# One of two modulation tables is computed on VectorE and ScalarE inside a feed-forward, instead of on TensorE inside a recurrent branch

## The chip, the cores and the metric

The kernel runs on one core of a Trainium2 chip. The metric is the device time of one execution in microseconds (us). The core has TensorE (matmuls into PSUM banks), VectorE, ScalarE and GpSimd; SyncE issues the weight transfers here. In the profile they are PE (with PEld for weight loads), DVE, ACT, POOL and SP.

## The reference, cut to what matters

Two network blocks of two layers each work one after the other on 256 tokens of width 1024. Block 1 mixes three branches (A is a delta-rule recurrence of many 64x64 products) and has a gated feed-forward. Block 2 modulates its norms and residual gates by tables that depend only on the condition `c`:

```python
cond = jax.nn.silu(c)
for layer in range(DEPTH):
    mod = (cond @ ada_w[layer] + ada_b[layer])[:, None, :]
    sh1, sc1, g1, sh2, sc2, g2 = jnp.split(mod, 6, axis=-1)
    h = rms_norm_2(x, norm_mix_g[layer]) * (1.0 + sc1) + sh1
    x = x + g1 * hybrid_mixer(h, ...)
    h = rms_norm_2(x, norm_ffn_g[layer]) * (1.0 + sc2) + sh2
    y = swiglu(h, ...) if layer % 2 == 0 else moe_swiglu(h, ...)
    x = x + g2 * y
```

`c` is one vector of 1024 and `ada_w[layer]` is 1024 x 6144, 25 MB in float32. The products `cond @ ada_w[0]` and `cond @ ada_w[1]` can be made at any time before block 2 needs them.

## The kernel before, in words

**Units.** All weights stream through the core in units of 128 x 1024 float32 (512 KB), in an order fixed by the table `ORDER.loads`. The SyncE program `weight_program` issues them in that order into a ring of 6 slots. Load n goes into the slot of load n-6 and waits until that older unit has been read for the last time.

**Split units (kind "s").** ScalarE copies a unit into `w_high` in a rounded form (`high_to`, L1713). VectorE makes `w_low` = unit minus `w_high` (`low_to`, L2235), and this frees the ring slot (semaphore `s_low_halves`). TensorE then multiplies high by high, high by low and low by high, 24 matmuls of 256 columns for one unit. There are 6 places for split units in `w_high`, so `high_to` also waits for TensorE to have multiplied the unit 6 before.

**Raw units (kind "r").** These are read by TensorE straight from the ring. In each of block 1's two layers, 48 of them make one modulation table. `mod_point` (L867) is called at 17 or more points of branch A, between its products. A point takes up to 4 raw units, two matmuls each (128 partitions by 32 columns, 512 wide). After each round of 16 units, ScalarE copies the bank out (`full`), a later point transposes it (`turned`, L872) and ScalarE takes the columns (`out`). The next round waits for `out`. At branch A's end VectorE copies the finished 48 columns into `raw_mod`.

**Feed-forward of block 2, layer 0.** Its 66 split units are 22 groups j of two up units and one down unit. TensorE takes up(j), then down(j-2). In group j ScalarE first cuts the units up to `fed_ahead(j)` (three new units for each group from the third on), then makes sigmoid(gate) (L2032), waits for VectorE's products, and rounds the hidden tile (`high`, L2036). VectorE makes the three `w_low`, two products (L2267) and the low part of the hidden tile. Engines work in program order, so a wait holds everything behind it on that engine.

Of the kernel before, what the change touches and what calls it, by code (L numbers as in the profile page):

```python
# [3 lines left out]
P = 128  # L4
# [107 lines left out]


class Order:

# [3 lines left out]
    LAYER1 = FEED + 3 * FF_GROUPS  # L119
    RAW1 = MOD_UNITS + 1  # L120
    QK2, RQK2, RV2, GV2, GR2, RG2, OUT2, FEED2 = 0, 4, 12, 16, 20, 24, 28, 36

    def __init__(self):
        self.loads = []
        for layer in range(LAYERS):
            self._load("s", self.layer1(layer), self.A_V)
            self._load("r", layer * self.RAW1, 1)
            self._load("s", self.layer1(layer) + self.A_V, self.C - self.A_V)
            self._load("r", layer * self.RAW1 + 1, MOD_UNITS)
# [41 lines left out]
    @staticmethod  # L171
    def fed_ahead(j, groups):

        return 5 if j == 0 else min(3 * j + 4, 3 * groups - 1)

    def layer1(self, layer):
# [70 lines left out]

class Rounds:

    ROUND = 2 * KT

    def __init__(self):
        self.taken, self.stage = 0, 0

    def more(self, n):
        r, at = self.stage // 3, self.stage % 3
        if at == 1:
            self.stage += 1  # L260
            return r, True, range(0)
        if at:
            return r, False, range(0)
        first, self.taken = self.taken, min(self.taken + n, (r + 1) * self.ROUND, MOD_UNITS)
        return r, False, range(first, self.taken)

    def out(self):
        r, at = self.stage // 3, self.stage % 3
        if (at == 0 and self.taken == (r + 1) * self.ROUND) or at == 2:
            self.stage += 1  # L270
            return r, at
        return r, None

    def open(self):
        return self.stage < 3 * MOD_UNITS // self.ROUND


STEPS = {
# [6 lines left out]
    "mod_act":  # L285
        "full0 out0 full1 out1 full2 out2",
    "a_pe":
# [14 lines left out]
    "b_pe":  # L302
# [150 lines left out]
def build(nc, a_x, a_pos, a_cond, a_const, a_par1, a_par2, a_router, a_norms, a_weights, a_moe, a_out):  # L453
# [163 lines left out]
    for w in tmps:  # L617
# [48 lines left out]
    CG, CV, SG, HD = ([new(T) for _ in TWO] for _ in range(4))  # L666


    space(0)
# [58 lines left out]
    of_start = stage("start", 0)  # L728
    of_mod, of_a, of_b, of_c, of_merge, of_ffn, of_add = (
        [stage(name, layer) for layer in range(LAYERS)]  # L730
        for name in ("mod", "a", "b", "c", "merge", "ffn", "add"))
    of_mix = [stage("first", 0), stage("mix", 0)]
# [53 lines left out]
    def tensor_program():  # L786
# [80 lines left out]
        def mod_point(M, A, rounds, layer, n=4):  # L867
            r, turn, units = rounds.more(n)
            if turn:
                pe.wait_ge(*M.act(f"full{r}"))  # L870
                for i in range(4):
                    ins = pe.transpose(psum[7][:, i * P:(i + 1) * P], rope[:, i * P:(i + 1) * P], c_("ident"))  # L872
                ins.then_inc(*M.pe.mark(f"turned{r}"))
            for j in units:
                k, block = j % Rounds.ROUND // 2, j % 2
                if j % Rounds.ROUND == 0:
                    pe.wait_ge(*(M.act(f"out{r - 1}") if r else A.dve("kk_scaled")))
                raw = layer * ORDER.RAW1 + 1 + j
                pe.wait_ge(*arrived("r", raw))
                for h in TWO:  # L880
                    q = 2 * block + h
                    ins = mm(psum[7][32 * q:32 * q + 32, :], cond[:, k:k + 1].to_broadcast([P, 32]),
                             weights("r", raw)[:, h * 512:(h + 1) * 512], k == 0, k == KT - 1)
                ins.then_inc(s_raw, 1)
            rounds.out()

        def branch_a(R, A, M, side, layer):
            s0, rounds, VT = ORDER.layer1(layer), Rounds(), PA[:, 8:12, :]
            point = lambda: mod_point(M, A, rounds, layer)
# [40 lines left out]
            ins.then_inc(*A.pe.mark("kk_sum"))  # L930
            low = layer * ORDER.RAW1
            lora = weights("r", low)
# [770 lines left out]
    def scalar_program():  # L1703
# [69 lines left out]
        def branch_a(A, M, side, layer):  # L1773
            s0, a, rounds = ORDER.layer1(layer), A.act, Rounds()
            WA, GD = PA[:, 12, :], PA[:, 13, :]

            def point():
                rounds.more(4)
                r, step = rounds.out()
                if step == 0:  # L1780
                    act.wait_ge(s_raw, layer * ORDER.RAW1 + (r + 1) * Rounds.ROUND + 1)
                    act.activation(rope, psum[7][:, :], Copy).then_inc(*M.act.mark(f"full{r}"))
                elif step == 2:
                    act.wait_ge(*M.pe(f"turned{r}"))
                    src = psum[7][:, :].rearrange("p (i q s) -> p q i s", i=4, q=4)[:, :, :, 0:1]
                    dst = mod[:, 16 * r:16 * r + 16].rearrange("p (q i o) -> p q i o", q=4, o=1)
                    act.activation(dst, src, Copy).then_inc(*M.act.mark(f"out{r}"))
# [31 lines left out]
            tiles_in(10, 14)  # L1819
            act.wait_ge(s_raw, layer * ORDER.RAW1 + 1)  # L1820
            for b in TWO:
# [193 lines left out]

        def feed_forward(F, s0, groups, conv=None, ahead=False, rotary=None):
            for j in range(groups):
# [186 lines left out]
        for layer in range(LAYERS):  # L2204
# [9 lines left out]
            if layer == 0:  # L2214
                feed_forward(of_feed, s0 + ORDER.FEED2, FF_GROUPS, ahead=True)
        route(of_route)
# [9 lines left out]
    def vector_program():  # L2226
# [114 lines left out]
        def branch_a(A, M, side, layer):  # L2341
# [436 lines left out]

        def feed_forward(F, S, s0, groups, conv=None, scale=None, ahead=False, rotary=None):
            for j in range(groups):  # L2780
# [325 lines left out]
        def modulation(S, layer):  # L3106
            d = S.dve
            tt(d, mod, raw_mod[:, layer * MOD_UNITS:(layer + 1) * MOD_UNITS], par2(layer, "ada_b"), ADD)
            prior(d)
# [29 lines left out]
        for layer in range(LAYERS):  # L3139
# [9 lines left out]
            if layer == 0:  # L3149
                feed_forward(of_feed, of_add2, s0 + ORDER.FEED2, FF_GROUPS, scale=lambda dt: mod[:, 40 + dt:41 + dt],  # L3150
                             ahead=True)
        route(of_route)
# [4 lines left out]
    def weight_program():  # L3157
# [3 lines left out]
        for n, (kind, unit) in enumerate(ORDER.loads):  # L3161
# [51 lines left out]
def weight_units(inp):  # L3213
# [3 lines left out]
    for l in range(LAYERS):  # L3217
# [3 lines left out]
        index = np.concatenate([c[:, 1024:1092], np.zeros((D, 60), np.float32)], 1)  # L3221
        mod = inp["ada_w_2"][l].reshape(KT, P, MOD_UNITS // KT, UNIT).transpose(2, 0, 1, 3).reshape(MOD_UNITS, P, UNIT)
        gates = columns(w[:, B_END + 1092:])
        raw += [low] + [mod[2 * KT * r + KT * b + k] for r in range(3) for k in range(KT) for b in range(2)]
        a_units = columns(w[:, :A_END])
# [7 lines left out]
    for l in range(LAYERS):  # L3233
# [7 lines left out]
    assert len(split) == ORDER.experts and len(raw) == LAYERS * ORDER.RAW1  # L3241
    return np.stack([(split if kind == "s" else raw)[n] for kind, n in ORDER.loads if kind == "r" or n < ORDER.experts])

# [67 lines left out]
```

## Time and profile before

| | |
|---|---|
| median of 3 runs | 2488.91 us (2483.47 to 2493.6) |
| the profiled execution's own time | 2488.56 us |
| its span | 2487.1 us |
| TensorE busy | 2289.8 us, 92% of the span |
| VectorE busy | 1600.5 us, 64% |
| ScalarE busy | 1177.9 us, 47% |
| weights and constants read | 423.08 MB |

Busy time is an average over stages with different limits: what an edit is worth is read in its own stage. In lists of instructions, the bracket at the end is the idle time of the engine just ahead of the row, with what ended it. A float32 matmul appears as two rows, so `x16` for raw units is 4 units.

### The profile page before, as it was taken

What the parts mean: (1) busy time and instruction counts of PE and PEld (TensorE: products, weight loads), DVE (VectorE), ACT (ScalarE), POOL (GpSimd) and SP (SyncE); (2) the same over time, 40 slices, a digit from 0 to 9 for tenths busy, and PEclk for the clock granted to TensorE, in tenths of its full rate; (3) what the DMA queues carried; (4) which work ended last, traced back from release to release, by engine and by line L of the source; (5) the groups of instructions that cost most, each with busy time, mean ns of one, the idle gap of its engine ahead of it and who ended that gap; (6) DMA issues with size and microseconds to landing.
All of it is one profiled execution on the core that took longest, in us unless ns stands there. A gap on an engine that the chain in (4) does not pass through costs nothing.

```text
span 2487.1 us, 44944 instructions
## 1 busy us (share of the span) xinstructions
PE 2289.8 (92%) x19043; PEld 2067.2 (83%) x19043; DVE 1600.5 (64%) x2429; ACT 1177.9 (47%) x1713; POOL 0.2 (0%) x4
## 2 busy tenths in 40 slices
PE   7889788999999888889999989999989999999998
PEld 7569788999976788888998979998978888887776
DVE  6537776687772687576875756555755554477886
ACT  5234534455552354355554435444434443356665
POOL 0000000000000000000000000000000000000000
PEclk9999898999999999899998979999978999999999
DMA  5664333355457533243653415563412455578895
GB/s 204 226 250 160 114 107 114 127 197 195 143 181 265 185 119 111 93 161 128 204 188 110 136 51 179 182 190 129 136 35 102 169 181 184 195 248 325 321 331 196
DMA packets 118635, 427.06 MB, mean 172 GB/s; under 512 B 13345, under 2 KB 16161, under 8 KB 118305
## 3 DMA queue, kind: packets, MB, share of 16 engines
q1 hardware_dynamic: 116016, 421.81, 49.5%
q8 instruction: 150, 2.46, 0.4%
q10 hardware_dynamic: 2416, 2.37, 0.3%
q14 instruction: 53, 0.43, 0.1%
HBM read 423.08 MB, written 1.05 MB: 171 GB/s over the span
## 4 chain that ended last, share of the span: by engine, by line
PE 75%; DVE 15%; ACT 5%; issue 3%; DMA 2%; SPq 0%; ACTq 0%; DVEq 0%
PE bank L790 74%; DVE w_low L2235 5%; DVE arena L2267 4%; DVE arena L2276 2%; DMA ring<-in_weights 1%; ACT w_high L1713 1%; DVE y_mix L2267 1%; DVE arena L2748 1%; DVE arena L2273 1%; PE bank L1599 1%; ACT arena L1986 1%; DVE small L2746 0%; DVE arena L2286 0%; DVE arena L2271 0%; ACT arena L1931 0%
## 5 line engine op out<-in xcount | busy, mean ns | idle before, releaser
L2235 DVE TENSOR_TENSOR w_low<-ring,w_high 128x1024 fp32r<-128x1024 f32 x700 | 823.3, 1220 | 159.4 <-ACT w_high L1713 159.0
L1713 ACT ACTIVATE w_high<-ring 128x1024 fp32r<-128x1024 f32 x700 | 700.3, 1051 | 166.2 <-PE bank L790 159.3
L790 PE MATMUL bank<-u_high,w_high 128*128 128x256 f32 x2576 | 745.9, 290 | 34.9 <-DVE u_low L2267 24.0
L790 PE MATMUL bank<-u_low,w_high 128*128 128x256 f32 x2576 | 737.3, 286 | 0.0
L790 PE MATMUL bank<-u_high,w_low 128*128 128x256 f32 x2576 | 736.5, 286 | 0.0
L790 PEld LDWEIGHTS bank<-u_high,w_high 128*128 128x128 f32 x2576 | 502.1, 195 | 48.3 <-issue 40.0
L790 PEld LDWEIGHTS bank<-u_low,w_high 128*128 128x128 f32 x2576 | 501.8, 195 | 0.1
L790 PEld LDWEIGHTS bank<-u_high,w_low 128*128 128x128 f32 x2576 | 500.9, 194 | 0.0
L790 PE MATMUL bank<-arena 64*64 64x64 f32 (+5 forms) x4456 | 245.1, 252 | 76.9 <-issue 20.1
L790 PEld LDWEIGHTS bank<-arena 64*64 64x64 f32 (+2 forms) x4456 | 215.0, 156 | 115.1 <-issue 60.6
L2267 DVE TENSOR_TENSOR arena<-arena 128x256 f32<-128x256 f32 (+3 forms) x218 | 141.8, 666 | 46.7 <-ACT arena L2030 21.3
L790 PE MATMUL bank<-w_high,u_high 128*128 128x256 f32 (+1 forms) x480 | 164.9, 344 | 0.0
L790 PE MATMUL bank<-w_high,u_low 128*128 128x256 f32 (+1 forms) x480 | 162.6, 339 | 0.0
L790 PE MATMUL bank<-w_low,u_high 128*128 128x256 f32 (+1 forms) x480 | 162.3, 338 | 0.0
L790 PE MATMUL bank<-hid_high,w_high 128*128 128x256 f32 x528 | 147.7, 280 | 0.9 <-DVE w_low L2235 0.9
L790 PE MATMUL bank<-hid_low,w_high 128*128 128x256 f32 x528 | 147.3, 279 | 0.0
L790 PE MATMUL bank<-hid_high,w_low 128*128 128x256 f32 x528 | 147.3, 279 | 0.0
L2267 DVE TENSOR_TENSOR turned_low<-bank,turned_high 128x256 fp32r<-128x256 f32 (+1 forms) x66 | 24.9, 400 | 158.7 <-ACT turned_high L2142 158.7
L2142 ACT ACTIVATE turned_high<-bank 128x256 fp32r<-128x256 f32 (+1 forms) x66 | 22.2, 365 | 220.8 <-PE bank L1599 220.8
L1719 ACT ACTIVATE arena<-bank 128x512 f32<-128x512 f32 (+1 forms) x72 | 42.1, 585 | 164.7 <-PE bank L790 164.6
L2276 DVE SCALAR_TENSOR_TENSOR arena<-bank,params,arena 128x255 f32<-128x255 f32 (+1 forms) x204 | 85.5, 476 | 42.8 <-ACT arena L2028 26.2
L790 PE MATMUL bank<-w_high,turned_high 128*128 128x512 f32 x242 | 99.6, 412 | 8.5 <-DVE w_low L2235 7.1
(294 smaller groups left out, 3068.6 us busy)
## 6 DMA issues: line engine op xcount, KB each, us to landing
ring<-in_weights SPq DMA_DIRECT2D x534, 512.0 KB, 4.5
ring<-in_moe SPq DMA_DIRECT2D x264, 512.0 KB, 5.3
const<-in_const SPq DMA_DIRECT2D x1, 2619.0 KB, 16.7
out<-x_res ACTq DMA_DIRECT2D x2, 512.0 KB, 3.0
x_res<-in_x SPq DMA_DIRECT2D x1, 512.0 KB, 5.0
x_res<-in_x ACTq DMA_DIRECT2D x1, 512.0 KB, 5.5
const<-in_par ACTq DMA_DIRECT2D x1, 462.0 KB, 3.4
params<-in_par ACTq DMA_DIRECT2D x1, 247.0 KB, 10.3
```

The source lines that it names most:

```text
L790: return pe.matmul(out, lhsT, rhs, start=start, stop=stop, skip_group_check=loose)
L1599: ins = pe.transpose(bank(q, tile)[:, f * P:(f + 1) * P], hid_e[q % 2][tile][:, f * P:(f + 1) * P], c_("ident"))
L1713: act.activation(WH[:, ORDER.slot[cut], :], weights("s", cut), Copy).then_inc(s_hi, 1)
L1719: act.activation(job.dst, held(job), Copy).then_inc(s_out["act"], 1)
L1986: act.activation(L_c[a][:, h, :], L_c[a][:, h, :], Exp, bias=neg_max[a][:, h:h + 1], accum_out=exp_sum[a][:, h:h + 1]).then_inc(*c.mark(f" ...
L2142: act.activation(HTH[q % 2][tile][:, 0:n], psum[4 + 2 * (q % 2) + tile][:, 0:n], Copy)\
L2235: dve.tensor_tensor(WL[:, b, :], weights("s", cut), WH[:, b, :].bitcast(f32), SUB).then_inc(s_lo, 1)
L2267: dve.tensor_tensor(out, a, b, op).then_inc(*t.mark(name))
L2273: dve.tensor_scalar(out, a, s1, s2, op0, op1).then_inc(*t.mark(name))
L2276: dve.scalar_tensor_tensor(out, a, s, b, op0, op1).then_inc(*t.mark(name))
L2748: dve.match_replace(work_[:, a, 0:n], top8, work_[:, a, 0:n], -3e30).then_inc(*d.mark())
```

## The change

The table of layer 0 is still made on TensorE in branch A, but in three rounds spread over both layers of block 1: rounds 0 and 1 (32 units) in layer 0, round 2 (16 units) in layer 1. Before, each layer made a whole table of 48 units.

The table of layer 1 leaves TensorE. Its weights are stored transposed (output columns on partitions), so that a column of the table is a row-wise sum of products. They are a new kind "m": unit m0 is `c` itself on all partitions, m1 to m48 are the weights. In block 2's first feed-forward, VectorE multiplies unit m_i by silu(c) in place in the ring, after the hidden tile of group j (`products(j)`). ScalarE then copies the unit onto itself with a sum over the row (`accum_out`), at the end of its next group (`sums(j-1)`). That sum frees the ring slot. `modulated(j)` gives 2 units to 15 of the groups 1 to 21 and 3 units to groups 4, 7, 11, 14, 18 and 21. The units m(j) are loaded right behind the split units that group j cuts.

```diff
 class Order:
-    RAW1 = MOD_UNITS + 1
+    ROUNDS1 = range(0, 2), range(2, 3)
...
-        for layer in range(LAYERS):
-            self._load("s", self.layer2(layer), self.FEED2 + (EXPERTS * EXPERT_UNITS if layer else 3 * FF_GROUPS))
+        self._load("s", self.layer2(0), self.FEED2)
+        for j in range(FF_GROUPS):
+            first, last = self.fed_ahead(j - 1, FF_GROUPS) + 1 if j else 0, self.fed_ahead(j, FF_GROUPS)
+            self._load("s", self.layer2(0) + self.FEED2 + first, last + 1 - first)
+            self._load("m", self.modulated(j)[0], len(self.modulated(j)))
+        self._load("s", self.layer2(1), self.FEED2 + EXPERTS * EXPERT_UNITS)
...
+    def modulated(j):
+        if j == 0:
+            return range(0, 1)
+        return range(1 + MOD_UNITS * (j - 1) // (FF_GROUPS - 1), 1 + MOD_UNITS * j // (FF_GROUPS - 1))
...
         def branch_a(R, A, M, side, layer):
-            s0, rounds, VT = ORDER.layer1(layer), Rounds(), PA[:, 8:12, :]
+            s0, rounds, VT = ORDER.layer1(layer), Rounds(ORDER.ROUNDS1[layer]), PA[:, 8:12, :]
...
-        def feed_forward(F, s0, groups, conv=None, ahead=False, rotary=None):
+        def feed_forward(F, s0, groups, conv=None, ahead=False, rotary=None, modulated=None):
+            def sums(j):
+                K = modulated
+                if j == 0:
+                    act.wait_ge(*arrived("m", 0))
+                    act.activation(cond_row, weights("m", 0), Sigmoid).then_inc(*K.act.mark("cond"))
+                for i in ORDER.modulated(j) if j else ():
+                    act.wait_ge(*K.dve(f"product{i}"))
+                    act.activation(weights("m", i), weights("m", i), Copy,
+                                   accum_out=raw_mod[:, MOD_UNITS + i - 1:MOD_UNITS + i]).then_inc(*K.act.mark(f"sum{i}"))
...
                 act.activation(HH[:, ts_], HD[n], Copy).then_inc(*f.mark("high"))
+                if modulated is not None and j != 1:
+                    sums(max(j - 1, 0))
...
+            if modulated is not None:
+                sums(groups - 1)
             if ahead:
                 high_to(s0 + 3 * groups + 2)
...
-            dve.wait_ge(*M.act("out2"))
-            copy(d, raw_mod[:, layer * MOD_UNITS:(layer + 1) * MOD_UNITS], mod)
...
+            def products(j):
+                K = modulated
+                if j == 0:
+                    dve.wait_ge(*K.act("cond"))
+                    tt(K.dve, cond_row, cond_row, weights("m", 0), MUL, "cond")
+                    prior(K.dve)
+                for i in ORDER.modulated(j) if j else ():
+                    dve.wait_ge(*arrived("m", i))
+                    tt(K.dve, weights("m", i), weights("m", i), cond_row, MUL, f"product{i}")
...
                 tt(f, HL[:, ts_], HD[n], HH[:, ts_].bitcast(f32), SUB, "hidden")
+                if modulated is not None:
+                    products(j)
...
                 old, was = ORDER.loads[n - RING]
-                sp.wait_ge(*((s_lo, was + 1) if old == "s" else (s_raw, was + 1)))
+                if old == "m":
+                    sp.wait_ge(*(of_modulated.act(f"sum{was}") if was else of_modulated.dve("cond")))
+                else:
+                    sp.wait_ge(*((s_lo, was + 1) if old == "s" else (s_raw, was + 1)))
```

TensorE's order in the middle of branch A of block 1's layer 1, before (`ring,cond` is a point with 4 raw units; L919 and L872 are transposes):

```order
L790 MATMUL bank<-arena 64x64 x32
L919 MATMUL bank<-const,arena 128x128 x4
L872 MATMUL bank<-const,rope 128x128 x4
L919 MATMUL bank<-const,arena 128x128 x4
L790 MATMUL bank<-const,arena 64x64 x16
...
L919 MATMUL bank<-const,arena 128x128 x4
L790 MATMUL bank<-ring,cond 32x512 x8
L790 MATMUL bank<-arena 64x64 x32
L790 MATMUL bank<-ring,cond 32x512 x8
L790 MATMUL bank<-arena 64x128 x32
L790 MATMUL bank<-arena 64x64 x32
L790 MATMUL bank<-ring,cond 32x512 x8
```

The same place now:

```order
L819 MATMUL bank<-arena 64x64 x32
L948 MATMUL bank<-const,arena 128x128 x8
L819 MATMUL bank<-const,arena 64x64 x16
L819 MATMUL bank<-arena 64x64 x16
L819 MATMUL bank<-const,arena 64x64 x16
L819 MATMUL bank<-arena 64x64 x16
L948 MATMUL bank<-const,arena 128x128 x4
L819 MATMUL bank<-arena 64x64 x32
L819 MATMUL bank<-arena 64x128 x32
L819 MATMUL bank<-arena 64x64 x272
```

The points are gone from here on, and the branch's own products stand back to back.

ScalarE's order in two groups of block 2's feed-forward, before (`s_slot` is the arrival of a unit, `s_units_multiplied` TensorE's progress):

```order
L1713 ACTIVATE w_high<-ring 128x1024 [waits s_units_multiplied,s_slot2]
L1713 ACTIVATE w_high<-ring 128x1024 [waits s_units_multiplied,s_slot3]
L1713 ACTIVATE w_high<-ring 128x1024 [waits s_units_multiplied,s_slot4]
L2032 ACTIVATE arena<-bank 128x256 [waits s_feed_dve,s_units_multiplied]
L2036 ACTIVATE hid_high<-arena 128x256 [waits s_units_multiplied,s_feed_dve]
L1713 ACTIVATE w_high<-ring 128x1024 [waits s_units_multiplied,s_slot5]
L1713 ACTIVATE w_high<-ring 128x1024 [waits s_units_multiplied,s_slot0]
L1713 ACTIVATE w_high<-ring 128x1024 [waits s_units_multiplied,s_slot1]
```

The same place now:

```order
L1742 ACTIVATE w_high<-ring 128x1024 [waits s_units_multiplied,s_slot5]
L1742 ACTIVATE w_high<-ring 128x1024 [waits s_units_multiplied,s_slot0]
L1742 ACTIVATE w_high<-ring 128x1024 [waits s_units_multiplied,s_slot1]
L2071 ACTIVATE arena<-bank 128x256 [waits s_feed_dve,s_units_multiplied]
L2075 ACTIVATE hid_high<-arena 128x256 [waits s_units_multiplied,s_feed_dve]
L2053 ACTIVATE ring,raw_mod<-ring 128x1024 [waits s_modulated_dve] x2
L1742 ACTIVATE w_high<-ring 128x1024 [waits s_units_multiplied,s_slot4]
L1742 ACTIVATE w_high<-ring 128x1024 [waits s_units_multiplied,s_slot5]
L1742 ACTIVATE w_high<-ring 128x1024 [waits s_units_multiplied,s_slot0]
```

Two or three sums now stand between a hidden tile and the next three cuts.

SyncE's order in the same stretch now, with what each transfer waits for (before, all of these waited for `s_low_halves`):

```order
L3236 DMA ring<-in_weights 128x1024 [waits s_low_halves] x3
L3236 DMA ring<-in_weights 128x1024 [waits s_modulated_act] x2
L3236 DMA ring<-in_weights 128x1024 [waits s_low_halves] x3
L3236 DMA ring<-in_weights 128x1024 [waits s_modulated_act] x2
L3236 DMA ring<-in_weights 128x1024 [waits s_low_halves] x3
L3236 DMA ring<-in_weights 128x1024 [waits s_modulated_act] x3
```

Where both neighbours have two m units, the second transfer of such a pair is the next group's first split unit; all transfers behind it on the queue wait with it.

## Rows read from the trace of the kernel before

**Rows 1.** The page: span, and the chain that ended last by engine.

```profile
span 2487.1 us, 44944 instructions
...
PE 75%; DVE 15%; ACT 5%; issue 3%; DMA 2%; SPq 0%; ACTq 0%; DVEq 0%
```

**Rows 2.** Busy time by window: the steady feed-forward of block 2 (stretch, length, engines, clock).

```profile
1531.00:1700.00 169.00, 169.00 (x1435) 169.00 (x1433) 98.96 (x123) 78.42 (x104) 0.00 (x0) 1.00 0.59 187
```

**Rows 3.** Timeline of TensorE in branch A, layer 1: points (start, length).

```profile
763.10 1.92 PE L790 MATMUL bank<-ring,cond 128*32 128x512 f32 x16
...
767.90 2.90 PE L790 MATMUL bank<-ring,cond 128*32 128x512 f32 x16
...
771.81 1.53 PE L790 MATMUL bank<-ring,cond 128*32 128x512 f32 x8
...
775.09 1.05 PE L790 MATMUL bank<-ring,cond 128*32 128x512 f32 x4 [0.20 <-DMA ring<-in_weights]
...
786.23 0.66 PE L872 MATMUL bank<-const,rope 128*128 128x128 f32 x4 [1.18 <-ACT rope L1782]
...
792.55 1.92 PE L790 MATMUL bank<-ring,cond 128*32 128x512 f32 x16 [0.76 <-ACT mod L1787]
...
796.42 1.94 PE L790 MATMUL bank<-ring,cond 128*32 128x512 f32 x12
...
813.96 3.55 PE L790 MATMUL bank<-ring,cond 128*32 128x512 f32 x16
```

**Rows 4.** Timeline of VectorE and ScalarE there: results that TensorE needs next.

```profile
768.02 0.69 DVE L2279 COPY arena<-bank 128x512 f32<-128x512 f32 x1 [0.24 <-PE bank L790]
...
785.10 0.60 ACT L1803 ACTIVATE arena<-bank 128x512 f32<-128x512 f32 x1 [3.85 <-PE bank L919]
...
796.54 0.69 DVE L2267 TENSOR_TENSOR arena<-bank,arena 128x512 f32<-128x512 f32 x1 [0.24 <-PE bank L790]
```

**Rows 5.** Waits of TensorE, 720 to 830 us: total, times, longest.

```profile
PE bank L790 <- issue: 9.4, 5, 4.1
```

**Rows 6.** Timeline of ScalarE and VectorE in block 2's feed-forward.

```profile
1537.00 0.37 ACT L2032 ACTIVATE arena<-bank 128x256 f32<-128x256 f32 x1
...
1559.76 0.39 ACT L2032 ACTIVATE arena<-bank 128x256 f32<-128x256 f32 x1 [1.73 <-PE bank L790]
1560.18 0.88 DVE L2267 TENSOR_TENSOR arena<-arena,bank 128x256 f32<-128x256 f32 x2 [0.88 <-ACT arena L2032]
1561.09 0.42 ACT L2036 ACTIVATE hid_high<-arena 128x256 fp32r<-128x256 f32 x1 [0.94 <-DVE arena L2267]
...
1561.54 0.43 DVE L2267 TENSOR_TENSOR hid_low<-arena,hid_high 128x256 fp32r<-128x256 f32 x1 [0.49 <-ACT hid_high L2036]
1562.49 2.46 DVE L2235 TENSOR_TENSOR w_low<-ring,w_high 128x1024 fp32r<-128x1024 f32 x2 [0.52 <-ACT w_high L1713]
...
1565.47 1.06 ACT L1713 ACTIVATE w_high<-ring 128x1024 fp32r<-128x1024 f32 x1 [1.79 <-PE bank L790]
1566.57 1.23 DVE L2235 TENSOR_TENSOR w_low<-ring,w_high 128x1024 fp32r<-128x1024 f32 x1 [1.62 <-ACT w_high L1713]
1568.26 0.39 ACT L2032 ACTIVATE arena<-bank 128x256 f32<-128x256 f32 x1 [1.73 <-PE bank L790]
```

**Rows 7.** Transfers into the ring, 1531 to 1700 us.

```profile
DMA to landing us min/median/max: 3.1/4.1/5.8
```

**Rows 8.** Rate of the transfers, 720 to 830 us, in 40 slices.

```profile
GB/s 241 401 419 417 401 383 225 7 209 396 164 86 270 352 67 6 168 402 393 407 380 411 182 311 346 74 6 287 402 369 401 271 398 165 12 237 317 215 6 0
```

**Rows 9.** Groups of instructions: ScalarE's sums over a row.

```profile
L1986 ACT ACTIVATION_READ_ACCUMULATOR arena<-arena,small 128x1 f32 x32 | 6.0, 187 | 0.0
```

**Rows 10.** Timeline at the feed-forward's end: last hidden tile, table load, squares.

```profile
1697.54 0.43 DVE L2267 TENSOR_TENSOR hid_low<-arena,hid_high 128x256 fp32r<-128x256 f32 x1 [0.49 <-ACT hid_high L2036]
...
1700.37 1.28 ACT L1742 ACT_TABLE_LOAD   x1
...
1702.59 3.16 ACT L1745 ACTIVATE arena<-x_res 128x256 f32<-128x256 f32 x8 [0.72 <-DVE x_res L2276]
```

More of the change, by code:

```diff
@@ L111, in constants, with __init__, more, out @@
     return c
+class Rounds:
+    ROUND = 2 * KT
+    def __init__(self, rounds):
+        self.first, self.last = rounds[0], rounds[-1] + 1
+        self.taken, self.stage = self.ROUND * self.first, 3 * self.first
+    def more(self, n):
+        r, at = self.stage // 3, self.stage % 3
+        if at == 1:
+            self.stage += 1
+            return r, True, range(0)
+        if at:
+            return r, False, range(0)
+        first, self.taken = self.taken, min(self.taken + n, (r + 1) * self.ROUND, self.last * self.ROUND)
+        return r, False, range(first, self.taken)
+    def out(self):
+        r, at = self.stage // 3, self.stage % 3
+        if (at == 0 and self.taken == (r + 1) * self.ROUND) or at == 2:
+            self.stage += 1
+            return r, at
+        return r, None
+    def open(self):
+        return self.stage < 3 * self.last
 class Order:
@@ L245, in made @@
         return jobs
[L248 to L275, printed above, removed]
 STEPS = {
@@ L728, in build @@
     of_start = stage("start", 0)
-    of_mod, of_a, of_b, of_c, of_merge, of_ffn, of_add = (
+    of_mod, of_modulated = [stage("mod", 0)] * LAYERS, stage("modulated", 0)
+    of_a, of_b, of_c, of_merge, of_ffn, of_add = (
         [stage(name, layer) for layer in range(LAYERS)]
-        for name in ("mod", "a", "b", "c", "merge", "ffn", "add"))
+        for name in ("a", "b", "c", "merge", "ffn", "add"))
     of_mix = [stage("first", 0), stage("mix", 0)]
@@ L876, in mod_point @@
                 if j % Rounds.ROUND == 0:
-                    pe.wait_ge(*(M.act(f"out{r - 1}") if r else A.dve("kk_scaled")))
-                raw = layer * ORDER.RAW1 + 1 + j
+                    pe.wait_ge(*(M.act(f"out{r - 1}") if r > rounds.first else A.dve("kk_scaled")))
+                raw = ORDER.raw1(layer) + 1 + j - rounds.first * Rounds.ROUND
                 pe.wait_ge(*arrived("r", raw))
@@ L930, in branch_a @@
             ins.then_inc(*A.pe.mark("kk_sum"))
-            low = layer * ORDER.RAW1
+            low = ORDER.raw1(layer)
             lora = weights("r", low)
@@ L1773, in branch_a @@
         def branch_a(A, M, side, layer):
-            s0, a, rounds = ORDER.layer1(layer), A.act, Rounds()
+            s0, a, rounds = ORDER.layer1(layer), A.act, Rounds(ORDER.ROUNDS1[layer])
             WA, GD = PA[:, 12, :], PA[:, 13, :]
@@ L1780, in point @@
                 if step == 0:
-                    act.wait_ge(s_raw, layer * ORDER.RAW1 + (r + 1) * Rounds.ROUND + 1)
+                    act.wait_ge(s_raw, ORDER.raw1(layer) + (r + 1 - rounds.first) * Rounds.ROUND + 1)
                     act.activation(rope, psum[7][:, :], Copy).then_inc(*M.act.mark(f"full{r}"))
@@ L1819, in branch_a @@
             tiles_in(10, 14)
-            act.wait_ge(s_raw, layer * ORDER.RAW1 + 1)
+            act.wait_ge(s_raw, ORDER.raw1(layer) + 1)
             for b in TWO:
@@ L2214, in scalar_program @@
             if layer == 0:
-                feed_forward(of_feed, s0 + ORDER.FEED2, FF_GROUPS, ahead=True)
+                feed_forward(of_feed, s0 + ORDER.FEED2, FF_GROUPS, ahead=True, modulated=of_modulated)
         route(of_route)
@@ L2777, in branch_c, with feed_forward @@
             branches_b_c(B, C, G, level, probabilities, side, layer, last)
-        def feed_forward(F, S, s0, groups, conv=None, scale=None, ahead=False, rotary=None):
+        def feed_forward(F, S, s0, groups, conv=None, scale=None, ahead=False, rotary=None, modulated=None):
+            def products(j):
[7 more added lines that the diff above has]
+                    tt(K.dve, weights("m", i), weights("m", i), cond_row, MUL, f"product{i}")
             for j in range(groups):
@@ L3107, in modulation @@
             d = S.dve
+            dve.wait_ge(*(of_modulated.act(f"sum{MOD_UNITS}") if layer else of_mod[0].act("out2")))
             tt(d, mod, raw_mod[:, layer * MOD_UNITS:(layer + 1) * MOD_UNITS], par2(layer, "ada_b"), ADD)
@@ L3150, in vector_program @@
                 feed_forward(of_feed, of_add2, s0 + ORDER.FEED2, FF_GROUPS, scale=lambda dt: mod[:, 40 + dt:41 + dt],
-                             ahead=True)
+                             ahead=True, modulated=of_modulated)
         route(of_route)
@@ L3221, in weight_units @@
         index = np.concatenate([c[:, 1024:1092], np.zeros((D, 60), np.float32)], 1)
-        mod = inp["ada_w_2"][l].reshape(KT, P, MOD_UNITS // KT, UNIT).transpose(2, 0, 1, 3).reshape(MOD_UNITS, P, UNIT)
+        mod = inp["ada_w_2"][0].reshape(KT, P, MOD_UNITS // KT, UNIT).transpose(2, 0, 1, 3).reshape(MOD_UNITS, P, UNIT)
         gates = columns(w[:, B_END + 1092:])
-        raw += [low] + [mod[2 * KT * r + KT * b + k] for r in range(3) for k in range(KT) for b in range(2)]
+        raw += [low] + [mod[2 * KT * r + KT * b + k] for r in ORDER.ROUNDS1[l] for k in range(KT) for b in range(2)]
         a_units = columns(w[:, :A_END])
@@ L3240, in weight_units @@
                          inp["ffn_w2_2"][0].reshape(FF_GROUPS, P, D))
-    assert len(split) == ORDER.experts and len(raw) == LAYERS * ORDER.RAW1
-    return np.stack([(split if kind == "s" else raw)[n] for kind, n in ORDER.loads if kind == "r" or n < ORDER.experts])
+    row = [np.broadcast_to(inp["c_2"][0], (P, UNIT)), *inp["ada_w_2"][1].T.reshape(MOD_UNITS, P, UNIT)]
+    assert len(split) == ORDER.experts and len(raw) == LAYERS + MOD_UNITS
+    of = {"s": split, "r": raw, "m": row}
+    return np.stack([of[kind][n] for kind, n in ORDER.loads if kind != "s" or n < ORDER.experts])
 def expert_units(inp):
```

12 lines of the change are left out of this document (9 added, 3 removed), and 10 rows, old and new, of the table STEPS.

## The prediction

> **What bounds the kernel now.** I read the chain that ended last first: three quarters of it is TensorE and little is DMA [rows 1]. So work taken off TensorE is worth time only where TensorE is what the stage waits for, and work put on other engines costs nothing only while it stays behind TensorE. Two stages are touched, and I read each in windows and then in its timeline.
>
> In block 2's first feed-forward, TensorE is busy for every microsecond of 169, at full clock; VectorE is busy for 99.0 of them and ScalarE for 78.4 [rows 2]. The sigmoids of successive groups stand 8.5 us apart (1559.76 and 1568.26), so one group of three units takes 8.5 us and one unit 2.83 us [rows 6]. In branch A, TensorE alternates between short products that wait on VectorE and ScalarE, and the points with raw units [rows 3].
>
> **What leaves branch A.** Layer 0 keeps 32 of 48 raw units, layer 1 keeps 16. The first four points of layer 1, which also wait most for transfers, and one turning stay. What follows is removed. For each place I take TensorE's time of the point and subtract what it would then wait for, since a point covers the latency of the other engines. In layer 1:
>
> - Three points of 1.92 us (4 units; one row stands for them) with nothing late behind them: 5.8.
> - The points at 767.90 and at 771.81, the latter with waits for transfers until 775.09 + 1.05: 2.9 + 4.3 = 7.2 [rows 3]. Between them TensorE needs VectorE's copy that began at 768.02 [rows 4]. VectorE's four instructions ahead of that copy then bind: I put the wait that appears at 1.4. Gain 5.8.
> - The turning at 786.23: its wait of 1.18 and about 0.5 of transposes go, but the next transpose must wait for ScalarE's copy, which starts when TensorE is ready (785.10) and takes 0.60 [rows 4]: with the hand-over 1.7 - 0.7 = 1.0.
> - The point at 792.55 with its wait of 0.76: 2.6.
> - The point at 796.42 (three units 1.94, the fourth another 1.05): 3.0, less 0.8 until VectorE's sum of 796.54 + 0.69 is there: 2.2.
> - The point at 813.96, which ran at half clock: 3.55, less 0.6 for VectorE's next results: 2.9.
> - The last turning hides a VectorE step and gives 0.
>
> Sum 20.3. In layer 0 the last four points go, in the same places: 2.6 + 2.2 + 1.9 + (1.9 - 0.6) = 8.0. Branch A gives 28.3 us. Bounds: TensorE also has idle pieces of "issue", where nothing in the profile holds it, five of them with 9.4 us in this stretch [rows 5]. They follow fast runs of small products. If they are instruction supply, removing the slow points lets them grow, and I take 10 off: 18. If they come from the transfers beside them, which stop earlier now, the longest (4.1) could shrink by 3, and all covers could be real gain: 38.
>
> **What is added to the feed-forward: busy time.** For 48 units, VectorE does one more 128x1024 operation (1.23 as `w_low`) and ScalarE one of 1.05 with a read of the accumulator of 0.19 [rows 6, 9], 1.24 together. Per group that is 2.3 x 1.23 = 2.8 on VectorE, which already works 0.88 + 0.43 + 3 x 1.23 = 5.0: 7.8 of 8.5 us. ScalarE comes to 4.0 + 2.8 = 6.8. By busy time alone both still fit behind TensorE, and a group with three units overruns VectorE by only 0.2. The 25 MB more take 60 us of wire, and the wire is 59% busy for 169 us, so this fits too, just.
>
> **What is added: a closed loop through the ring.** This is where I part from the busy times. The ring has 6 slots and each group now loads 5 (3 split, 2 m). The load 6 places behind a group's first split unit is the last m unit two groups back: in SyncE's order, the pair that waits for `s_modulated_act`. That m unit is released by a sum at the end of ScalarE's group j, and the split unit loaded on it is the first thing ScalarE cuts in group j+1. So nothing can be ahead. Counted from the last sum of a group:
>
> 1. The transfer lands after 3.2 (the least is 3.1 [rows 7]); two more follow at 0.52 MB / 419 GB/s = 1.25 each [rows 8]: 5.7.
> 2. ScalarE cuts the third unit: 1.05, at 6.8. VectorE makes its low half, 1.23 plus hand-over, at 8.0. The sigmoid is hidden beside it.
> 3. VectorE's two products 0.9, ScalarE's rounding 0.45 [rows 6]: 9.4.
> 4. Two sums of 1.24: 11.9, and the next transfer starts.
>
> So a group takes 11.9 us instead of 8.5. With three m units there is one more transfer ahead and one more sum: 14.4. TensorE's lead (a unit's low half is ready about 10 us ahead of its use) does not help: the loop does not contain TensorE, and the last hidden tile is on it. TensorE's 8.5 us of work leave it idle 3.4 us in each group; at half clock for part of it, it still keeps up, because its sigmoid input is wanted 10 us later.
>
> The loop starts with the sums of group 2. Its sigmoid is at 1537.00 [rows 6], so the sums end at 1537.0 + 1.8 + 2.5 = 1541.3. To the sums of group 20 there are 18 passes, 5 of them with three: 18 x 11.9 + 5 x 2.5 = 226.7. Then group 21's only split unit: 3.2 + 1.05 + 1.23 + 0.9 + 0.45 + 0.45 = 7.3. The last hidden tile is done at 1775.3 instead of 1698.0 [rows 10]: +77.3. At the end, three products (3.7) and the last sum stand ahead of the residual and of three cuts (3.2), the table load (1.3) and the squares (3.2): I find 13.5 from hidden tile to the last square against 7.8 now [rows 10], +5.7. The feed-forward costs +83. Bounds: with the median landing of 4.1 in place of 3.2, and 0.4 more in hand-overs, each of 18 passes takes 1.3 more, +23, so 106; if transfers land in their least time and half of ScalarE's and VectorE's steps overlap better, 0.7 less in each pass, 70.
>
> A rule speaks for the change here. The Trainium skill (DMA: Bandwidth & Descriptors, Rules for kernel authors) says to issue a transfer early and wait late, so that its fixed cost is overlapped. By it, with a ring of six, the landing would be hidden, the added cost 0 and the total about 2460. The trace shows that hiding today, since no engine waits for a transfer in this feed-forward; whether it lasts is what the slot's release decides.
>
> **Sum.** 2488.6 (the profiled execution's own time, 0.3 under the median of the runs) - 28.3 + 83 = 2543. The smallest difference that a measurement of this kernel can tell from none is about 0.5%, 12 us.
>
> **The rivals.**
>
> - Closed loop at the prices above: 2543, own range 2522 to 2560. Chance 0.70.
> - The same loop, dearer: landings of 4.1 and more, since bursts of four transfers follow each release. 83 + 23 = 106: 2566. For it speaks the median [rows 7]; against it, that the wire is idle when the first transfer of a burst starts. Chance 0.15.
> - The loop is loose: the slot is in truth free before ScalarE comes round, and the work hides behind TensorE's 8.5 us. Then only branch A's gain stays: 2488.6 - 28.3 = 2460, faster. The point from which this decides: the passes must average under 8.5 + 28.3 / 19 = 10.0 us. For it speak the busy times and TensorE's lead of 10 us; against it the order of sums, releases and cuts, which no duration changes. The skill's rule above is this rival. Chance 0.08.
> - A half-way case: passes of about 10 us, because transfers and cuts overlap more than I allow, or groups with three m units break the loop. It ends near 2490 to 2515. Chance 0.07.
>
> **Range and chances.** 2515 to 2570 leaves out the loose loop, part of the half-way case and the dearest loop, 2 in 10. Slower by over 0.5% (above 2501): the two loops, 0.85, and half of the half-way case, 0.03: 0.88. Within 0.5%: 0.04. Faster: 0.08.
>
> **What the profile after would show.** Branch A of layer 1 shorter by 20 us and of layer 0 by 8. In the feed-forward, sigmoids 11.9 us apart (14.4 in five places); TensorE busy about 70%, waiting for `w_low`; ScalarE's cuts waiting for the DMA of `ring`, which they don't do now; SyncE waiting for ScalarE's sums. If sigmoids stay 8.5 us apart, the loop is wrong. If TensorE's idle "issue" in branch A grows by as much as the points gave, the first term is wrong. If the cuts wait but less than 1.5 us in a group, landings are hidden better than I think.

## The result, and the profile after

The changed kernel takes 2572.56 us (median of 4 runs, 2567.48 to 2579.92), the kernel before 2487.24 us in the same comparison. The ratio is 1.0339 with a 95% interval of 1.032 to 1.0358: 3.4% slower, some 85 us. The forecast was 2543 with a range of 2515 to 2570, so the sign and the mechanism came out, and the size fell outside, by 2.6 us at the median.

The page of the changed kernel, span and the chain that ended last (against [rows 1]); the profiled execution took 2579.92 us:

```profile
span 2578.5 us, 44675 instructions
...
PE 65%; DVE 17%; ACT 8%; DMA 6%; issue 3%; SPq 1%; ACTq 0%; DVEq 0%
PE bank L819 64%; DMA ring<-in_weights 6%; DVE w_low L2278 6%; DVE arena L2310 5%; ACT w_high L1742 2%; ACT ring L2053 2%; DVE arena L2319 1%; DVE y_mix L2310 1%; DVE arena L2789 1%; SPq L3236 1%; PE bank L1628 1%; ACT arena L2015 1%; DVE arena L2316 0%; DVE small L2787 0%; DVE arena L2329 0%
```

TensorE holds 10 points less of the chain. Transfers into the ring have entered it, with SyncE's issue and ScalarE's sums (L2053). The same windows view as [rows 2], of the feed-forward from its third to its 21st sigmoid:

```profile
1506.00:1768.00 262.00, 185.13 (x1307) 181.44 (x1306) 137.22 (x151) 111.85 (x172) 0.00 (x0) 0.85 0.55 191
```

TensorE is busy for 71% of it where it was busy for all, and its mean granted clock is 0.85 where it was 1.00. No other engine took over: VectorE is busy 52%, ScalarE 43%, the wire 55%. Where nothing is busy all the time, the waits have to be read. They close in a circle (who waited for whom, total, times, longest; engines first from 1500 to 1790 us, then SyncE's queue from 1506 to 1768):

```profile
ACT w_high L1742 <- DMA ring<-in_weights: 123.3, 54, 7.3
...
PE bank L819 <- DVE w_low L2278: 76.9, 18, 7.0
...
SPq L3236 <- ACT ring L2053: 218.8, 41, 13.5
```

ScalarE's cuts wait for transfers, the transfers' queue waits for ScalarE's sums, and TensorE waits for what comes of the cuts. One pass, in ScalarE's timeline:

```profile
1609.42 0.36 ACT L2071 ACTIVATE arena<-bank 128x256 f32<-128x256 f32 x1
1611.59 0.42 ACT L2075 ACTIVATE hid_high<-arena 128x256 fp32r<-128x256 f32 x1 [1.80 <-DVE arena L2310]
1611.91 1.04 ACT L2053 ACTIVATE ring<-ring 128x1024 f32<-128x1024 f32 x1
1612.86 0.19 ACT L2053 ACTIVATION_READ_ACCUMULATOR ring<-ring 128x1 f32 x1
1612.95 1.04 ACT L2053 ACTIVATE ring<-ring 128x1024 f32<-128x1024 f32 x1
1613.90 0.19 ACT L2053 ACTIVATION_READ_ACCUMULATOR ring<-ring 128x1 f32 x1
1619.21 1.06 ACT L1742 ACTIVATE w_high<-ring 128x1024 fp32r<-128x1024 f32 x1 [5.13 <-DMA ring<-in_weights]
1620.78 1.06 ACT L1742 ACTIVATE w_high<-ring 128x1024 fp32r<-128x1024 f32 x1 [0.51 <-DMA ring<-in_weights]
1622.07 1.06 ACT L1742 ACTIVATE w_high<-ring 128x1024 fp32r<-128x1024 f32 x1 [0.24 <-DMA ring<-in_weights]
1623.04 0.36 ACT L2071 ACTIVATE arena<-bank 128x256 f32<-128x256 f32 x1
```

From sigmoid to sigmoid 13.6 us, where [rows 6] have 8.5. The sigmoid (L2071) follows the last cut at once; no wait for TensorE stands at it. After the second sum ScalarE stands 5.1 us until the split unit that took that slot has landed.

Branch A, TensorE's timeline in layer 1 in the middle and at the end of the branch (against [rows 3]), and the wait for issue there, 700 to 815 us, and in layer 0, 60 to 180 us (against [rows 5]):

```profile
771.43 5.83 PE L819 MATMUL bank<-arena 64*64 64x128 f32 x202 [0.50 <-DVE arena L2310]
777.96 1.97 PE L819 MATMUL bank<-arena 64*64 64x64 f32 x114 [0.70 <-issue]
780.20 0.46 PE L819 MATMUL bank<-arena 64*64 64x64 f32 x14 [0.26 <-ACT arena L1904]
781.88 1.49 PE L819 MATMUL bank<-arena 64*64 64x64 f32 x66 [1.23 <-issue]
...
792.12 1.97 PE L819 MATMUL bank<-y_mix,const 128*128 128x256 f32 x8 [1.34 <-DVE y_mix L2322]
```

```profile
PE bank L819 <- issue: 6.5, 4, 2.5
...
PE bank L819 <- issue: 6.8, 4, 2.7
```

The row of 792.12 stood at 827.58 before, and the last one alike in layer 0 went from 178.43 to 162.07. The points are gone, and the idle issue time shrank too: from 9.4 to 6.5 us in layer 1, and from 10.7 to 6.8 us in layer 0. This difference scatters: with the same branch A the same windows show 8.3 and 6.1 us in `a_only` below, and 7.3 and 7.5 in `beside`.

### The profile page after: what moved, and what is told of

Its sections match the earlier page's. It is cut to its first block, busy times and chain, and to the rows that moved or that the text cites. A ratio compares the mean times of both kernels' runs of the same rounds, so it can differ in the third digit from the quotient of the medians.

```text
span 2578.5 us, 44675 instructions
## 1 busy us (share of the span) xinstructions
PE 2300.0 (89%) x18839; PEld 2096.3 (81%) x18839; DVE 1656.8 (64%) x2476; ACT 1226.0 (48%) x1804; POOL 0.2 (0%) x4
## 3 DMA queue, kind: packets, MB, share of 16 engines
HBM read 423.60 MB, written 1.05 MB: 165 GB/s over the span
## 4 chain that ended last, share of the span: by engine, by line
PE 65%; DVE 17%; ACT 8%; DMA 6%; issue 3%; SPq 1%; ACTq 0%; DVEq 0%
PE bank L819 64%; DMA ring<-in_weights 6%; DVE w_low L2278 6%; DVE arena L2310 5%; ACT w_high L1742 2%; ACT ring L2053 2%; DVE arena L2319 1%; DVE y_mix L2310 1%; DVE arena L2789 1%; SPq L3236 1%; PE bank L1628 1%; ACT arena L2015 1%; DVE arena L2316 0%; DVE small L2787 0%; DVE arena L2329 0%
## 5 line engine op out<-in xcount | busy, mean ns | idle before, releaser
L819 PE MATMUL bank<-u_high,w_high 128*128 128x256 f32 x2576 | 759.1, 295 | 111.8 <-DVE w_low L2278 81.1
L819 PE MATMUL bank<-u_low,w_high 128*128 128x256 f32 x2576 | 747.9, 290 | 0.0
L819 PE MATMUL bank<-u_high,w_low 128*128 128x256 f32 x2576 | 747.0, 290 | 0.0
L819 PEld LDWEIGHTS bank<-u_high,w_high 128*128 128x128 f32 x2576 | 513.1, 199 | 128.6 <-DVE w_low L2278 86.0
L819 PEld LDWEIGHTS bank<-u_low,w_high 128*128 128x128 f32 x2576 | 513.1, 199 | 0.1
L819 PEld LDWEIGHTS bank<-u_high,w_low 128*128 128x128 f32 x2576 | 512.1, 199 | 0.0
```

The costliest lines, as they stand in the source:

```text
L819: return pe.matmul(out, lhsT, rhs, start=start, stop=stop, skip_group_check=loose)
```

## The experiments

They ran in two sets, each beside the kernel before on one chip: `a_only`, `ffn_only`, `beside` and `short_m` with 2491.09 us for the kernel before, the other four with 2490.13 on another chip. The comparison of the result had 2487.24, so a difference between sets holds to some 4 us. Times are medians of 4 runs, 10 for the last. The edits are shown cut, with `...` where lines are left out.

**The theory.** The loss is a closed loop through the ring: a sum frees a slot, a split unit is loaded into it, ScalarE must cut that unit, and only behind the cuts and the hidden tile come the next sums. **Rivals:** VectorE or ScalarE has too much to do; the wire is too slow for 5 units a group; part of branch A's gain was given back elsewhere.

**1. Branch A's part alone (`a_only`).** The m units are neither loaded nor worked on; block 2 takes layer 0's table in both layers.

```diff
             self._load("s", self.layer2(0) + self.FEED2 + first, last + 1 - first)
-            self._load("m", self.modulated(j)[0], len(self.modulated(j)))
...
-            tt(d, mod, raw_mod[:, layer * MOD_UNITS:(layer + 1) * MOD_UNITS], par2(layer, "ada_b"), ADD)
+            tt(d, mod, raw_mod[:, 0:MOD_UNITS], par2(layer, "ada_b"), ADD)
...
```

> Leaves out the layer-1 table (its m units are neither loaded, multiplied nor summed; layer 0's table is used for both layers), and keeps the rounds of branch A as changed. Theory (all of the loss is in the feed-forward, and branch A gained what the start of the feed-forward shows, 33 us): 2487 - 33 = 2454, sigmoids of the feed-forward 8.5 us apart again. Rival (the gain in branch A is partly spent later whatever the feed-forward does): between 2460 and 2475.

Measured 2455.81, ratio 0.9856 (0.9824 to 0.9888): 35 us faster. The feed-forward is as it was before, TensorE busy in all of 169 us. Branch A's gain is real and nothing of it is spent later.

**2. The feed-forward's part alone (`ffn_only`).** Layer 0's table is made twice, in 48 units in each layer, as the work was before.

```diff
-    ROUNDS1 = range(0, 2), range(2, 3)
+    ROUNDS1 = range(0, 3), range(0, 3)
...
```

> Branch A as before (48 raw units in each layer, both for layer 0's table), and the feed-forward as changed. Theory (the two parts add): 2487 + 118 = 2605. Rival (the loop's cost depends on when the feed-forward starts or on what stands before it): off from that by more than 10 us.

Measured 2609.42, ratio 1.0482 (1.0437 to 1.0526): 118 us slower. 118 - 35 = 83, against 85 for the whole change. The parts add.

**3. Who frees the slot (`beside`).** Every product and sum of the change is made, but VectorE writes the product to one of four tiles in unused memory, so SyncE waits for the product and no longer for the sum.

```diff
+    beside = [at((30 + 4 * n) * T, 4 * T) for n in range(4)]
...
-                    act.activation(weights("m", i), weights("m", i), Copy,
+                    act.activation(beside[i % 4], beside[i % 4], Copy,
...
-                    tt(K.dve, weights("m", i), weights("m", i), cond_row, MUL, f"product{i}")
+                    if i > 4:
+                        dve.wait_ge(*K.act(f"sum{i - 4}"))
+                    tt(K.dve, beside[i % 4], weights("m", i), cond_row, MUL, f"product{i}")
...
-                    sp.wait_ge(*(of_modulated.act(f"sum{was}") if was else of_modulated.dve("cond")))
+                    sp.wait_ge(*of_modulated.dve(f"product{was}" if was else "cond"))
```

> All of the changed kernel's work, but VectorE writes each product to one of four tiles beside the ring, so that the product and not the sum frees the slot. Theory (closed loop: sum, transfer, cut, next sum): the loop is open, a group is back near 8.5 us, total 2454 to 2465. Rival (VectorE and ScalarE have too much to do, or the wire is too slow): a group stays above 11 us and the total above 2520.

Measured 2457.39, ratio 0.9861 (0.9832 to 0.9889): 34 us faster than before and 115 faster than the change. It does all the work of the reference and is the fastest of the kernels here that do. Its feed-forward in the windows view, its waits on transfers (1500 to 1690 us) and a stretch of ScalarE's timeline:

```profile
1506.00:1670.00 164.00, 162.08 (x1366) 161.87 (x1364) 142.70 (x168) 119.81 (x193) 0.00 (x0) 1.00 0.92 331
...
ACT w_high L1743 <- DMA ring<-in_weights: 2.2, 7, 1.1
```

```profile
1590.04 1.05 ACT L2054 ACTIVATE arena<-arena 128x1024 f32<-128x1024 f32 x1
1590.99 0.18 ACT L2054 ACTIVATION_READ_ACCUMULATOR arena<-arena 128x1 f32 x1
1591.08 2.94 ACT L1743 ACTIVATE w_high<-ring 128x1024 fp32r<-128x1024 f32 x3
```

The three cuts follow the last sum at once. VectorE is now busy 87%, the wire 92%, at full clock and 331 GB/s, and TensorE 99%. So the rivals of busy engines and of a slow wire fall, though VectorE and the wire have little left.

**4. No products (`no_products`).** VectorE's 48 products are left out; ScalarE sums the units as they land.

```diff
-                    act.wait_ge(*K.dve(f"product{i}"))
+                    act.wait_ge(*arrived("m", i))
...
-                for i in ORDER.modulated(j) if j else ():
-                    dve.wait_ge(*arrived("m", i))
-                    tt(K.dve, weights("m", i), weights("m", i), cond_row, MUL, f"product{i}")
```

> As changed, but VectorE's 48 products are left out: ScalarE sums the unit as it landed. Slots are still freed by the sums. Theory (VectorE is not on the loop): within 12 us of 2572. Rival (VectorE, at 7.8 of 8.5 us, is what makes the groups longer): 2500 or less.

Measured 2574.54, ratio 1.0341 (1.032 to 1.0362). No change within the noise: VectorE's added work is not on the loop.

**5. No sums (`no_sums`).** ScalarE's sums are left out, the product in place frees the slot, and both layers use layer 0's table.

```diff
-                    act.activation(weights("m", i), weights("m", i), Copy,
-                                   accum_out=raw_mod[:, MOD_UNITS + i - 1:MOD_UNITS + i]).then_inc(*K.act.mark(f"sum{i}"))
...
-                    sp.wait_ge(*(of_modulated.act(f"sum{was}") if was else of_modulated.dve("cond")))
+                    sp.wait_ge(*(of_modulated.dve(f"product{was}" if was else "cond")))
...
```

> As changed, but ScalarE's 48 sums are left out and VectorE's product in place frees the slot; layer 0's table is used for both layers. Theory (who frees the slot decides): no loop, 2454 to 2462 as in the kernel with tiles beside the ring. Rival (the 5 transfers a group cannot keep up with six slots): over 2480.

Measured 2453.68, ratio 0.9854 (0.9829 to 0.9879). This alone would also fit "ScalarE is too busy"; with experiment 3, where ScalarE makes all the sums at the same total within 4 us, it does not.

**6. Sums earlier (`sums_early`).** ScalarE makes the sums behind the sigmoid, before it waits for the hidden tile.

```diff
+                if modulated is not None and j > 1:
+                    sums(j - 1)
                 act.wait_ge(*F[j].dve("product"))
...
-                if modulated is not None and j != 1:
-                    sums(max(j - 1, 0))
+                if modulated is not None and j == 0:
+                    sums(0)
```

> As changed, but ScalarE makes the sums of the group before right after the sigmoid, ahead of the rounding of the hidden tile, instead of behind it. Theory (the pass is a chain: sum, transfers, cuts, products, rounding, sums): VectorE's products and the rounding, 2.4 us between the last cut and the first sum, leave the chain; a pass goes from 14.6 to some 12.2, total 2572 - 19 x 2.4 = 2526. Rival (throughput of an engine or of the wire sets the pass): no change, 2572.

Measured 2534.91, ratio 1.0189 (1.0167 to 1.021): 38 us less than the change, 2.0 a pass instead of the 2.4 expected; in the two profiled executions the 18 passes average 12.1 against 14.6 us, which is 2.4. The same instructions in another order are worth 38 us: a chain explains that, and the busy time of an engine or of the wire does not. ScalarE's timeline shows the sums next to the sigmoid. From the last sum to the first cut it still takes 4.6 to 7.0 us, 5.6 in the mean of 18 passes, against 5.8 in the changed kernel:

```profile
1600.34 0.37 ACT L2071 ACTIVATE arena<-bank 128x256 f32<-128x256 f32 x1
1600.60 1.05 ACT L2053 ACTIVATE ring<-ring 128x1024 f32<-128x1024 f32 x1
...
1602.59 0.19 ACT L2053 ACTIVATION_READ_ACCUMULATOR ring<-ring 128x1 f32 x1
1602.68 0.40 ACT L2077 ACTIVATE hid_high<-arena 128x256 fp32r<-128x256 f32 x1
1608.23 1.06 ACT L1742 ACTIVATE w_high<-ring 128x1024 fp32r<-128x1024 f32 x1 [5.14 <-DMA ring<-in_weights]
```

**7. Short m transfers (`short_m`).** Of each of the units m1 to m48 only 128 of 1024 columns are moved; the rest of the product and sum works on what the slot held.

```diff
+            if kind == "m" and unit:
+                sp.dma_start(ring[:, n % RING, 0:128], src[:, 0:128]).then_inc(s_slot[n % RING], 16)
+                continue
             sp.dma_start(ring[:, n % RING, :], src).then_inc(s_slot[n % RING], 16)
```

> As changed, but only an eighth of the columns of each unit m1 to m48 is moved; all waits, products and sums stay. Theory (the pass is 14.6 us and not 12.6 since 2 or 3 m transfers share each burst with three split units): a pass loses some 2.3 x 1.3 us or more, 11 to 12 us, total 2500 to 2520. Rival (the extra 2 us are hand-overs or busy engines): within 10 us of 2572.

Measured 2536.32, ratio 1.0198 (1.0155 to 1.0241): 36 us less than the change, 1.9 a pass, and less than the 50 to 70 that I had expected. The loop stays and ScalarE's wait is shorter:

```profile
1602.66 0.18 ACT L2053 ACTIVATION_READ_ACCUMULATOR ring<-ring 128x1 f32 x1
1606.23 2.26 ACT L1742 ACTIVATE w_high<-ring 128x1024 fp32r<-128x1024 f32 x2 [3.38 <-DMA ring<-in_weights]
```

3.4 us from the last sum to the first cut here. Over the 18 passes it is 3.2 to 4.7, 3.7 in the mean, where the changed kernel has 5.8 and my sum had 3.2 (4.45 with three m units). A pass takes 12.7 us in the mean; the forecast had 12.6 and the changed kernel has 14.6. So nearly all of the difference between my pass and the real one is the m transfer that is still on the wire when the split unit is issued behind it.

**8. Tiny points (`tiny_points`).** The kernel before, but the raw units that the change moves away from branch A are multiplied in 16 of 512 columns. Their transfers and turnings stay.

```diff
+                    few = 16 if j >= (16 if layer else 32) else 512
-                    ins = mm(psum[7][32 * q:32 * q + 32, :], cond[:, k:k + 1].to_broadcast([P, 32]),
-                             weights("r", raw)[:, h * 512:(h + 1) * 512], k == 0, k == KT - 1)
+                    ins = mm(psum[7][32 * q:32 * q + 32, 0:few], cond[:, k:k + 1].to_broadcast([P, 32]),
+                             weights("r", raw)[:, h * 512:h * 512 + few], k == 0, k == KT - 1)
```

> The kernel before, but the raw units that the change takes out of branch A (the third round in layer 0, the second and third in layer 1) are multiplied in 16 of their 512 columns; their transfers and the turnings stay. Theory (branch A gave 33 us and not 28 since TensorE's idle time of instruction supply shrinks when the transfers beside it are gone): the idle issue time stays at 9 to 11 us in each layer, total near 2470. Rival (it shrinks for another reason): issue idle 6 to 7 us in each layer, total 2460.

Measured 2486.01, ratio 0.9979 (0.9966 to 0.9993): 4 us, where I had expected 20. The idle issue time did not shrink, as the theory said, but the total did not follow. TensorE's waits in layer 1 (720 to 830 us), and its timeline there:

```profile
PE bank L790 <- issue: 10.4, 8, 3.2
PE bank L790 <- DMA ring<-in_weights: 9.8, 8, 3.2
```

```profile
771.95 0.30 PE L790 MATMUL bank<-ring,cond 128*32 128x16 f32 x4 [1.03 <-DMA ring<-in_weights]
773.22 0.29 PE L790 MATMUL bank<-ring,cond 128*32 128x16 f32 x4 [0.97 <-DMA ring<-in_weights]
773.45 1.97 PE L790 MATMUL bank<-const,arena 64*64 64x64 f32 x32
```

A unit of 1.05 us became one of 0.3 us, but units still land 1.27 us apart. Waits for transfers in layer 1 grew from 2.0 to 9.8 us, issue stayed at 10.4 (12.2 in layer 0), and the mean clock of that stretch is 0.89. Taking only TensorE's columns away gives next to nothing, taking units with their transfers gives 35 us. How much of the rest is the transfers' pace and how much the lower clock, these runs don't separate.

## Why the prediction was right and wrong

**Right: the closed loop.** It was forecast at one place by one chain, from the ring's order and not from busy times. The chain of the changed kernel runs round it, experiments 3 and 5 open it, 4 leaves it, and 6 shortens it, as it demands. The kernel is slower, as forecast.

**Wrong: the price of step 1 of the loop.** "The transfer lands after 3.2" took the least landing for one transfer alone. But the transfer of an m unit had been issued one sum (1.04 us) earlier and had not landed, and where m(j) has three units a second one goes out directly ahead of the split unit. Measured from the last sum to the first cut: 5.0 to 5.6 us in an ordinary pass, 5.4 to 6.1 behind three sums, 6.3 to 7.3 where m(j) has three units; 5.8 in the mean of 18 passes, where the forecast had 3.2 and, in five of them, 4.45. The rest of the pass nearly came out: from the first cut to the end of the third 3.9 (forecast 3.6), from there to the end of the rounding 2.5 (forecast 2.6), two sums 2.1 (forecast 2.5). So an ordinary pass is 13.6 and not 11.9, and the mean over the passes is 14.6 and not 12.6. From the sigmoid of group 2 to the last hidden tile the forecast added 77.3 us and the trace shows 115 (1505.80 to 1781.85, against 1537.00 to 1697.97). Experiment 7 shows that the m transfers make nearly all of the difference: without seven eighths of their bytes the wait is 3.7 us in the mean and the pass 12.7.

I had given this case as "the same loop, dearer" with 0.15 and 2566 us, against it "that the wire is idle when the first transfer of a burst starts". That is true of the m unit, which goes first, and not of the split unit behind it, which ScalarE waits for. Its landing of 4.1 was still too small: between 1510 and 1770 us the median landing is 6.3. The kernel before already showed such a price, not in this feed-forward but in branch A, where transfers follow each other closely: from 720 to 830 us their median landing was 6.0.

**Undersized: branch A's gain**, 28.3 forecast, 35 measured (experiment 1). By layer, from the last point that both kernels have to the row of `y_mix` at the branch's end (first the kernel before, then the changed one, whose last row in layer 1 stands above):

```profile
132.68 1.92 PE L790 MATMUL bank<-ring,cond 128*32 128x512 f32 x16
162.32 1.40 PE L790 MATMUL bank<-arena 64*64 64x64 f32 x75 [1.44 <-issue]
172.86 4.61 PE L790 MATMUL bank<-arena 64*64 64x64 f32 x128 [2.77 <-issue]
178.43 1.97 PE L790 MATMUL bank<-y_mix,const 128*128 128x256 f32 x8 [0.96 <-DVE y_mix L2279]
749.95 1.92 PE L790 MATMUL bank<-ring,cond 128*32 128x512 f32 x16
827.58 1.96 PE L790 MATMUL bank<-y_mix,const 128*128 128x256 f32 x8 [0.96 <-DVE y_mix L2279]
...
129.00 1.92 PE L819 MATMUL bank<-ring,cond 128*32 128x512 f32 x16
151.63 1.61 PE L819 MATMUL bank<-arena 64*64 64x64 f32 x91 [1.52 <-issue]
162.07 1.97 PE L819 MATMUL bank<-y_mix,const 128*128 128x256 f32 x8 [1.22 <-DVE y_mix L2322]
734.79 1.92 PE L819 MATMUL bank<-ring,cond 128*32 128x512 f32 x16
```

In layer 1 the stretch went from 77.6 to 57.3 us: 20.3, the sum that the walk gave. In layer 0 it went from 45.8 to 33.1: 12.7, where the walk gave 8.0. `ffn_only` has the branch before and `a_only` the changed one: 78.6 and 58.6 us in layer 1, 47.0 and 32.6 in layer 0, the same picture. So the walk's sum was right in layer 1 and some 5 us short in layer 0. There the idle issue time of the stretch fell from 4.2 us to 1.5, which is over half of it; what made the rest stays open. The remaining 2 us are scatter: the stretch of layer 0 that the change leaves alone, from the first point on (66.55 to 132.68 before), took 66.1 us before, 61.7 after, and 59.8 in `tiny_points`, whose instructions there are those of the kernel before.

What the issue idle time is, the forecast left open between instruction supply and the transfers beside it. The trace settles the first half. The kernel's DMA has a queue `instruction`, which brings packets of 16 KB. In branch A of six kernels (before, after, `a_only`, `beside`, `ffn_only`, `tiny_points`) each of the 62 idle pieces put down to issue ends 1.15 to 1.61 us after such a packet ended. The longest one before, idle from 808.43 to 812.49, has its packet from 810.27 to 811.21 (the DMA view of 810.2 to 811.3 us: packets, MB, share of 16 engines):

```profile
q8 instruction: 1, 0.02, 5.3%
```

So TensorE waited for instructions there. That weight transfers beside it make these waits longer is not shown: the packets themselves took 0.9 to 1.1 us before and 0.9 to 1.4 after the change. Experiment 8 only shows that the idle time stays where the transfers stay.

**The end of the feed-forward.** Forecast 13.5 us from the last hidden tile to the last square, measured 13.6 (1781.85 to 1795.49).

**The sum.** In the rows of the profiled executions the sigmoid of group 2 comes 31.2 us earlier, the loop adds 115.1 and the end 5.9: +89.8, and their own times differ by 91.4, since the profiled execution of the changed kernel was the slowest of its four. With experiment 1's 35 the sum is -35 + 115 + 6 = 86, against 85 between the medians; that it agrees so closely is luck. The two errors of the forecast have opposite signs: branch A gave 7 us more, the loop cost 38 more.

**The loose loop as a rival**, 0.08, came true only where the product frees the slot (experiments 3 and 5): in experiment 3 the total is 34 us under that of the kernel before, and ScalarE's cuts wait 2.2 us in all for transfers. The Trainium skill (DMA: Bandwidth & Descriptors, Rules for kernel authors) says to issue a DMA early and wait on its semaphore late, so that the fixed cost is overlapped. In the changed kernel the trace doesn't agree, with 123.3 us of waits for transfers at the cuts: six slots don't let a transfer be issued early when its slot's releaser stands just ahead of its reader.

## What to carry to other kernels

When a new kind of tile goes into a shared ring, list for each load which instruction frees its slot and where the load's reader stands on the same engine. If the releaser comes just ahead of the reader in program order, each group pays transfer, reading and release in a row, whatever the busy times say. Free the slot with the first reader, by writing to other memory, and the same work is hidden. Price a landing inside such a loop with all transfers issued just ahead of it on the wire, by a stretch of the trace where transfers follow each other as closely.

## What the runs showed of the hardware

Small matmuls beside transfers: with the columns of 48 units reduced to 16, the total fell by only 4 us. From 720 to 830 us TensorE was busy for 86.2 us where it was busy for 92.4, waits for units that landed 1.27 us apart grew from 2.0 to 9.8 us, and the mean granted clock was 0.89 in place of 0.97. The 32 products after the last tiny unit of one point took 1.97 us where they took 1.15 before.

A sum over a row of 1024 cost ScalarE 1.04 us from one to the next, with the read of the accumulator (0.19) inside it and not behind it: I had counted 1.24.

Where two transfers of 512 KB were released one sum (1.04 us) apart, the second had landed 5.0 to 5.6 us after the end of the second sum. With the first cut to 64 KB it was 3.3 to 4.0 us.

TensorE stood still for 0.2 to 4.6 us at a time in runs of 64x64 products, and each time went on 1.15 to 1.61 us after a packet of 16 KB on the instruction queue had ended.
